# Merge and output projection for the sample's tiles first, the sample's top-k in two half lists beside the prompt's merge

## The reference, cut to what matters

```python
h  = RMSNorm(x) * (1 + scale1) + shift1
[qA|kA|vA|qB|kB|vB|gA|gB] = h @ w_in
oA = global GQA(...)  @ w_branch_a      # 8 heads of 64
oB = windowed GQA(...) @ w_branch_b
x  = x + gate1 * ((sigmoid(gA) * oA + sigmoid(gB) * oB) @ w_out)      # "merge", "output projection"
h2 = RMSNorm(x) * (1 + scale2) + shift2
# expert choice, each group routed as one set, 16 experts, cap = 2 n / 16 (32 and 128 tokens):
aff = softmax(h2 @ w_router);  g, idx = top_k(aff.T, cap)
hid = silu(h2[idx] @ w_e_gate) * (h2[idx] @ w_e_up)                  # D_FF = 2048
x  = x + gate2 * scatter_add(idx, (hid @ w_e_down) * g)
y  = RMSNorm(x)
```

## Time and profile before

| | us |
|---|---|
| Median of 3 runs (lowest, highest) | 2573.92 (2571.49, 2574.54) |
| The profiled execution | 2572.49 |
| Its span in the trace | 2570.7 |
| PE busy | 2384.8 (93%) |
| DVE busy | 1605.4 (62%) |
| ACT busy | 1162.8 (45%) |
| POOL busy | 1123.0 (44%) |
| Mean DMA rate | 199 GB/s |

### The profile page before, as it was taken

One profiled execution on the slowest core, in us unless ns is written; L12 is line 12 of the kernel. 1 busy time (PEld: TensorE's weight loads), 2 busy tenths in 40 slices (PEclk: granted clock), 3 DMA queues, 4 the chain that ended last, 5 costly groups with the idle time before them and its releaser, 6 DMA issues.

```text
span 2570.7 us, 53875 instructions
## 1 busy us (share of the span) xinstructions
PE 2384.8 (93%) x23508; PEld 1712.8 (67%) x23508; DVE 1605.4 (62%) x2014; ACT 1162.8 (45%) x1468; POOL 1123.0 (44%) x721
## 2 busy tenths in 40 slices
PE   8999899998999999934899999999999999999993
PEld 3444477655555555523788888888888888888871
DVE  1643466556111125575888878887888878887862
ACT  2111455567111112330656655665556655556552
POOL 0000111146232331042657667776677666676640
PEclk9999899999999999956999999999999999999997
DMA  8100300220221103252889998999899998999965
GB/s 315 33 17 1 115 1 1 99 99 2 82 50 50 25 34 115 99 207 76 300 317 330 324 318 321 326 336 320 312 331 318 343 315 317 331 330 326 315 234 188
DMA packets 230113, 512.23 MB, mean 199 GB/s; under 512 B 7819, under 2 KB 35580, under 8 KB 229756
## 3 DMA queue, kind: packets, MB, share of 16 engines
q1 hardware_dynamic: 219324, 477.36, 52.3%
q0 software_dynamic: 10560, 31.46, 4.4%
HBM read 480.49 MB, written 28.31 MB: 198 GB/s over the span
## 4 chain that ended last, share of the span: by engine, by line
PE 85%; DVE 6%; POOL 2%; SPq 2%; ACT 1%; DMA 1%; issue 1%; DVEq 0%; POOLq 0%; ACTq 0%
PE ps L1403 21%; PE ps L1404 20%; PE ps L1405 20%; PE ps L1472 7%; PE ps L1688 4%; PE ps L1533 3%; PE ps L1545 3%; PE ps L1514 2%; DVE arena L1054 1%; DVE ti_s L1063 1%; DVE top_s L1062 1%; DVE arena L1064 1%; POOL arena L679 1%; PE ps L1625 1%; POOL arena L676 1%
## 5 line engine op out<-in xcount | busy, mean ns | idle before, releaser
L1403 PE MATMUL ps<-arena 128*128 128x160 bf16 (+2 forms) x5344 | 1308.6, 264 | 21.8 <-DVE arena L1335 8.3
L1404 PE MATMUL ps<-arena 128*128 128x160 bf16 (+2 forms) x5344 | 1308.6, 264 | 0.0
L1405 PE MATMUL ps<-arena 128*128 128x160 bf16 (+2 forms) x5344 | 1308.4, 264 | 0.0
L1302 DVE TENSOR_TENSOR arena<-arena 128x2048 bf16<-128x2048 f32 x376 | 919.2, 2450 | 193.3 <-ACT arena L803 192.3
L803 ACT ACTIVATE arena<-arena 128x2048 bf16<-128x2048 f32 x384 | 726.7, 1904 | 239.0 <-PE ps L1405 176.9
L1403 PEld LDWEIGHTS ps<-arena 128*128 128x128 bf16 x5344 | 524.1, 98 | 154.6 <-issue 27.0
L1405 PEld LDWEIGHTS ps<-arena 128*128 128x128 bf16 x5344 | 524.3, 98 | 127.8 <-issue 1.9
L1404 PEld LDWEIGHTS ps<-arena 128*128 128x128 bf16 x5344 | 524.3, 98 | 118.9 <-issue 1.4
L727 POOL TENSOR_TENSOR arena<-arena 128x320 bf16<-128x320 f32 x128 | 283.8, 2217 | 10.0
L724 POOL TENSOR_TENSOR arena<-arena,ones 128x320 bf16<-128x320 f32 x128 | 179.4, 1401 | 179.3 <-DVE arena L1335 179.0
L991 ACT ACTIVATE arena<-ps 128x160 f32<-128x160 f32 x256 | 77.4, 303 | 351.4 <-PE ps L1405 351.4
(11 more groups left out here) (197 smaller groups left out, 2377.8 us busy)
## 6 DMA issues: line engine op xcount, KB each, us to landing
arena<-w_e_gate SPq DMA_DIRECT2D x64, 2048.0 KB, 9.1
arena<-w_e_up SPq DMA_DIRECT2D x64, 2048.0 KB, 9.5
arena<-w_e_down SPq DMA_DIRECT2D x64, 2048.0 KB, 9.2
arena<-w_ada SPq DMA_DIRECT2D x12, 2048.0 KB, 8.6
arena<-x_sample SPq DMA_DIRECT2D x16, 512.0 KB, 3.5
arena<-w_in SPq DMA_DIRECT2D x16, 512.0 KB, 5.3
arena<-w_in SPq DMA_DIRECT2D x3, 2048.0 KB, 21.0
arena<-w_out SPq DMA_DIRECT2D x2, 2048.0 KB, 8.0
```

The costliest lines, as they stand in the source:

```text
L1302: ve.tensor_tensor(lo, stage_half(kind, a), hi, ALU.subtract).then_inc(lo_done, 1)
L1403: pe.matmul(out, w_hi, x_hi, start=start, stop=False)
L1404: pe.matmul(out, w_hi, x_lo, start=False, stop=False)
L1405: return pe.matmul(out, w_lo, x_hi, start=False, stop=stop)
```

## The change

- The merge runs for the sample's tiles alone (`M, m, 0` and `M, m, 1`, 512 tokens each), then the sample's eight output projections, with all that follows each of them. Positions p = 0 to 9 stand for the tiles 2 to 9, 0, 1 (`tile_at`).
- The prompt's merge becomes steps `M2, m, b` (b = 0, 1 for the two branches) after the sample's projections, each 36 matmuls 256 wide with one sigmoid and one product. For it all eight weight tiles are loaded and split a second time (`WS, 8` to `WS, 15`): two within the sample's projections, six within the prompt's merge. Of these second splits POOL makes the low half of 2048 columns and DVE that of 1024.
- The sample's affinities lie as two lists of 512 columns, on partitions 0 to 15 and 32 to 47. The sixteen rounds (`KR`) run over 64 partitions x 512, two or three after each of the prompt's merge steps from m = 2 on. `KM` makes one list of the two sorted ones: the largest 128 are the elementwise larger of the first list and the second read backwards.
- Four `GT` steps move from the end into the prompt's merge steps m = 3 and 4.
- Two expert chunks are loaded within the prompt's merge; the first eight low halves are made by DVE, four before and four after it modulates expert 0's rows. POOL's loop for them is gone.
- The layouts of `qT`, `oT`, `hTs` and `mergedS` change so that the two groups lie apart.

The diff, cut to its core:

```diff
         s.append(("M", m, 0))
         if m + 1 < KD:
             s.append(("WS", m + 1))
-        s.append(("M", m, 1))
         if m == KD - 1:
             s += [("WO", 0), ("WO", 1)]
-        s.append(("M", m, 2))
-    for t in range(NT + 3):
-        if t < NT:
-            s.append(("O", t))
-        if t == 0:
+        s.append(("M", m, 1))
+    ns = NT - PT_TILES
+    for p in range(ns):
+        s.append(("O", p))
+        if p == 0:
             s += [("GT", n) for n in range(4)]
-        if 0 <= t - 1 < NT:
-            s.append(("X2", t - 1))
-        if 0 <= t - 2 < NT:
-            s.append(("RT", t - 2))
-        if 0 <= t - 3 < NT:
-            s.append(("AT", t - 3))
-        if t == 6:
-            s.append(("K", 0))
-        if t < NT:
-            s.append(("XO", t))
-    s += [("GT", n) for n in range(4, 8)]
-    s += [("K", 1), ("I",)]
+        if p >= 1:
+            s.append(("X2", p - 1))
+        if p >= 2:
+            s.append(("RT", p - 2))
+        if p >= 3:
+            s.append(("AT", p - 3))
+        s.append(("XO", p))
+        if p in (1, 3):
+            s.append(("WS", KD + p // 2))
+    tail = {(0, 1): [("X2", ns - 1), ("RT", ns - 2), ("AT", ns - 3)], (1, 0): [("RT", ns - 1), ("AT", ns - 2)],
+            (1, 1): [("AT", ns - 1)], (3, 0): [("GT", 4)], (3, 1): [("GT", 5)], (4, 0): [("GT", 6)], (4, 1): [("GT", 7)]}
+    r = 0
+    for m in range(KD):
+        for b in range(2):
+            s.append(("M2", m, b))
+            s += tail.get((m, b), [])
+        if m + 2 < KD:
+            s.append(("WS", KD + m + 2))
+        for _ in range((0, 0, 2, 3, 3, 3, 3, 2)[m]):
+            s.append(("KR", r))
+            r += 1
+    assert r == CAP_S // 8
+    s += [("O", ns), ("KM",), ("XO", ns), ("O", ns + 1), ("X2", ns), ("XO", ns + 1), ("RT", ns), ("AT", ns), ("X2", ns + 1),
+          ("RT", ns + 1), ("AT", ns + 1), ("K", 0), ("K", 1), ("I",)]
     return s
...
+            sp.wait_ge(mm_ready, 2 * KD)
             def load_chunk(d, c):
...
                 src = w_down[0, e].rearrange("(k p) n -> p k n", p=P)[:, 4 * DOWN[q]:4 * DOWN[q] + 4, :]
                 sp.dma_start(at(stage[kind], 4, D), src).then_inc(w_ld[kind], 16)
-            for t in range(2):
-                sp.dma_start(xo[:, t], token_rows(x_d, t)).then_inc(xo_in[t], 16)
-            for t in range(NT):
-                if t + 2 < NT:
-                    sp.wait_ge(x1_ready, t + 1)
-                    sp.dma_start(xo[:, t % 2], token_rows(x_d, t + 2)).then_inc(xo_in[t % 2], 16)
+            for p in range(2):
+                sp.dma_start(xo[:, p], token_rows(x_d, tile_at(p))).then_inc(xo_in[p], 16)
+            sp.wait_ge(wos_ready, 4)
+            mw_load(KD)
+            for p in range(NT - 2):
+                sp.wait_ge(x1_ready, p + 1)
+                sp.dma_start(xo[:, p % 2], token_rows(x_d, tile_at(p + 2))).then_inc(xo_in[p % 2], 16)
+                if p == 1:
+                    sp.wait_ge(ws_done, KD + 1)
+                    sp.wait_ge(ws_rest, 1)
+                    mw_load(KD + 1)
+            for k in range(2, KD):
+                sp.wait_ge(ws_done, KD + k)
+                sp.wait_ge(ws_rest, k)
+                mw_load(KD + k)
+                if k in (3, 4):
+                    sp.wait_ge(out_done, NT - PT_TILES)
+                    load_chunk(-1, k - 3)
             sp.wait_ge(out_done, NT)
-            load_chunk(-1, 0)
-            load_chunk(-1, 1)
             load_chunk(0, 2)
             for n, c in enumerate((3, 4, 6, 7, 9, 10)):
...
+                if k == "WS" and s[1] >= KD:
+                    m = s[1]
+                    gp.wait_ge(ws_hi, m + 1)
+                    w = half_words(mws2[m % 2], 2, MW)[:, :, 0:2 * KD * P]
+                    gp.tensor_tensor(w[:, 1], at(mw, 2 * KD * P), w[:, 0], ALU.subtract).then_inc(ws_rest, 1)
...
-            for h in range(AHEAD):
-                gp.wait_ge(hi_done, h + 1)
-                kind, slot = ring(first_half(h))
-                hi, lo = split_half(slot, h % 2)
-                gp.tensor_tensor(lo, stage_half(kind, h % 2), hi, ALU.subtract).then_inc(lo_done, 1)
             for b in range(2):
...
+                        ac.wait_ge(m_done, 2 * KD)
+                    elif m > KD:
+                        ac.wait_ge(m2_done, 2 * (m - KD) - 2)
                     ac.wait_ge(mw_in[m % 2], 96 * (m // 2 + 1))
-                    ac.activation(half_words(mws[m % 2], 2, MW)[:, 0], at(mw, MW), ACT.Copy).then_inc(ws_hi, 1)
+                    ac.activation(half_words((mws if m < KD else mws2)[m % 2], 2, MW)[:, 0], at(mw, MW), ACT.Copy)\
+                        .then_inc(ws_hi, 1)
                 if k == "WO":
                     h = s[1]
                     ac.wait_ge(wo_in[h], 16)
...
+                        ac.activation(sig[:, n % 2, b], ps[:, 4 * (n % 2) + b], ACT.Sigmoid).then_inc(sig_ready, 1)
+                if k == "M2":
+                    n, b = merge_part(s)[0], s[2]
+                    ac.wait_ge(m2_done, 2 * s[1] + b + 1)
+                    ac.wait_ge(merged_ready, n - 1)
+                    ac.activation(sig[:, n % 2, b, 0:SEQ], ps[:, 2 * (n % 2) + b, 0:SEQ], ACT.Sigmoid).then_inc(sig_ready, 1)
...
+                link(ve.max(v, a))
+                ve.max_index(ti[b][0:rows, r * 8:r * 8 + 8], v, a)
+                link(ve.match_replace(a, v, a, -1.0))
+            def merge_halves():
+                def backward(x):
...
+                first, pos = top[1][0:NE], tif[1][0:NE]
+                pick = late[0:NE, 2]
+                ve.tensor_tensor(pick, first, v, ALU.is_ge)
+                link(ve.tensor_tensor(pos, pos, f, ALU.subtract))
+                link(ve.tensor_tensor(pos, pos, pick, ALU.mult))
+                ve.tensor_tensor(first, first, v, ALU.max)
+                link(ve.tensor_tensor(pos, pos, f, ALU.add))
+            def topk_prompt():
+                for r in range(CAP_P // 8):
+                    top_round(0, r, affP[:])
+                link(ve.tensor_copy(tif[0][:], ti[0][:]))
+                ve.tensor_copy(top4, top[0][:].unsqueeze(1).to_broadcast([NE, 4, CAP_P]))
+                for g in range(4):
+                    ins = ve.tensor_scalar(tif4[:, g], tif[0][:], 4.0, float(g), ALU.mult, ALU.add)
+                link(ins)
                 ve.engine_nop().then_inc(topk_ready, 1)
             ve.memset(relb, NEG).then_inc(chain, 1)
             count[0] += 1
...
-                    w = half_words(mws[m % 2], 2, MW)
-                    ve.tensor_tensor(w[:, 1], at(mw, MW), w[:, 0], ALU.subtract).then_inc(ws_done, 1)
+                    a = 0 if m < KD else 2 * KD * P
+                    w = half_words((mws if m < KD else mws2)[m % 2], 2, MW)[:, :, a:]
+                    ve.tensor_tensor(w[:, 1], at(mw, MW)[:, a:], w[:, 0], ALU.subtract).then_inc(ws_done, 1)
                 if k == "WO":
                     h = s[1]
                     for q in range(2):
...
+                if k == "M2":
+                    n, b = merge_part(s)[0], s[2]
+                    ve.wait_ge(sig_ready, 2 * n + b + 1)
+                    x = sig[:, n % 2, b, 0:SEQ]
+                    ins = ve.tensor_tensor(x, x, ps[:, 2 * (n % 2) + b, SEQ:2 * SEQ], ALU.mult)
+                    if b:
+                        ins.then_inc(mm_ready, 1)
...
                 if k == "AT":
                     t = s[1]
                     b, free = job(s)
-                    if t < PT_TILES:
-                        dst = affP[:, t * P:(t + 1) * P]
+                    if t < NT - PT_TILES:
+                        if t == 0:
+                            link(ve.memset(affS, -1.0))
+                        dst = affS[32 * (t // 4):32 * (t // 4) + NE, t % 4 * P:(t % 4 + 1) * P]
...
-                if k == "K":
-                    topk(s[1], affP[:] if s[1] == 0 else affS)
+                if k == "KR":
+                    top_round(1, s[1], affS)
+                if k == "KM":
+                    merge_halves()
+                if k == "K" and s[1] == 0:
+                    topk_prompt()
                 if k == "I":
...
+            for h in range(4):
+                split_low(*ring(first_half(h)), h % 2, h + 1)
             for n in range(3):
                 modulate_rows(0, n, 0, first=True)
+            for h in range(4, AHEAD):
+                split_low(*ring(first_half(h)), h % 2, h + 1)
...
+                    t0 = PT_TILES + 4 * c
                     for b in range(2):
                         wb = [half_words(o + KD * P + NPAIR * P // 2 * b, NPAIR, P) for o in part]
-                        out = ps[:, 4 * (n % 2) + 2 + b, 0:w].rearrange("p (t q) -> p t q", q=P)
+                        out = ps[:, 4 * (n % 2) + 2 + b].rearrange("p (t q) -> p t q", q=P)
                         for kk in range(NPAIR):
                             ins = split_product(out, [x[:, kk, :] for x in wb],
-                                                [oT[:, NPAIR * b + kk, 4 * c:4 * c + w // P, q * P:(q + 1) * P]
```

(50 more changed lines are left out.)

145 lines of the change are left out of this document (70 added, 75 removed).

## The result

The changed kernel takes **2581.28 us** (median of 7 runs, 2580.34 to 2582.36), the kernel before 2573.92 (7 runs, 2570.56 to 2575.8): ratio 1.0032, 95% interval 1.0021 to 1.0042. It is slower, by about 7 us; forecast were 8 us less. The profiled executions lie 9.9 us apart, with spans of 2580.5 and 2570.7 us. Expert 0's first matmul stands at 1208.71 instead of 1198.96, 9.75 us later, and from there to the end both kernels need the same (1371.8 and 1371.7 us), so the whole difference lies ahead of it.

What follows compares the result with a forecast made beforehand. PE runs without a gap from expert 0's first matmul, so its start sets the end: merge start 998.8 + merge 126.5 + projections, tail, top-k 44.8 + turn 21.5 gives 1191.6, 7.4 us earlier. Forecast 2566 us, range 2552 to 2582.

Steps and rivals of the forecast that it cites:

- the turn: From the prompt's top-k end to expert 0's first matmul: 21.5 us forecast, 16.6 before, with DVE's low halves as the path.
- the prediction's signs of being wrong: Prompt's merge under 110 or over 135 us, POOL's 2048-wide subtraction over 6, turn over 28, or a longer expert 0.
- The rival that ends on the other side: At the turn to the experts, each of POOL's six row splits waits for a low half, +12.3 us: 2579, chance 0.17.
- The load turn: In the prompt's merge, one staging buffer makes load and splits run in series: 8.2 + 2.8 + 1.1 + 4.1 = 16.2 us.
- The detour: At m = 3 and 4, `GT` waits for DVE's diagonals and holds ACT's next weight copy: merge 126.5 us, 113 without cost.
- A single turn of the loop: One load, ACT high half, DVE and POOL low halves in the prompt's merge: 16.2 us, against 7.8 of PE.
- POOL's 2048-wide low half beside DVE's: In the prompt's merge, POOL's 4.06 us low half gives way to DVE's 1024 columns, so 1.1 us is added.
- that rival: Two to three rounds hold POOL's low half back at m = 4 to 7, +21 us: 2587, chance 0.05.
- The start of the merge: The prompt's merge begins at 998.8 us, after the sample's merge ends at 894.7 and its projections follow.
- Projections, tail and prompt's top-k: Between the prompt's merge and the turn: two projections 20.7 us, last tile's tail 17.9, top-k 6.2; 44.8 in all.
- The clock: PE's granted clock drops after idle stretches, adding 3.5 us to the last step of the prompt's merge.
- The rival asked for 0.50 throughout: PE's granted clock stays at 0.50 from m = 3 on and in the first projection, +5 us: 2571, chance 0.20.

## Why the prediction was wrong

**The step that failed is the turn**, in the sentence "A gather issued while DVE splits weights is a step that I price at nothing above, for it ends before DVE is through with its four low halves". The prediction took DVE's four low halves as the path and everything else as lying beside them. They took 8.9 us, as assumed, but they keep POOL from its two index copies as well as from the gathers: 5.5 us, shown by the kernel in which DVE waits. The rows then needed 7.15 us, not 3.73, since the low halves had released two 2 MB loads, one after the second and one after the fourth: shown by the kernel in which the chunks wait. No rival had this part. The last split met two low halves (4.0), not one (2.45). Forecast was 4.9 more than before; it is 12.7 by the prediction's own measure (29.3 against 16.6). Of the prediction's signs of being wrong two came: a turn over 28 us, and an expert 0 that takes longer than before (67.8 us to expert 1's first matmul against 67.0).

The rival that ends on the other side named this place and 2579, by the wrong sum: it had all six splits held and the gather at 0.5 in place of 5.5, and a chance of 0.17. The Trainium skill spoke against me here ("SBUF — State Buffer", section on SBUF's two separate sides): of a GpSimd instruction that reads SBUF and a DVE one with two SBUF inputs, the one that starts first has the shared port pair for its whole length. Trace and experiment agree, index copies of 32x1 included (2.06 us beside a low half, 0.18 without). I should have asked which instructions of POOL stand behind a low half, not only the large ones.

**The load turn was mis-sized, in three of six.** This is a term of the sum, not the mechanism. "8.2 us with the signal" was read from a load that had the queues to itself. The load of m = 2, issued beside row writes and an x load, took 13.2 us until ACT's copy; those of m = 3, 4 and 7 took 10.2, 8.4 and 10.6. With m = 3's weights ready at 44.3 us into the merge instead of 37.4, all that follows is 6 to 8 late, and the end is 6.8 late. Most of it is the load of m = 2: asked for early, it makes the merge 5.8 us shorter and the kernel 4.9 faster. Why those of m = 3 and 7 took so long stays open. In five other kernels that load m = 3, 4 and 7 in the same way they took 8.2 to 9.4 us, beside the same chunk load for m = 3; and no other load was issued beside m = 7's, in the changed kernel either.

**What held.** The detour: 13.5 forecast; taking it out shortened the merge by 14.8, 11 to 13 of them in the two turns that hold it. A single turn of the loop: 16.2 forecast, 16.3 to 17.0 measured without the detour. The round on 512 columns: 2.15 forecast, 2.16 measured; POOL's 2048-wide low half beside DVE's: 5.16 forecast, 5.10 measured, and never held by a round, so that rival falls. The start of the merge lies within its scatter. Projections, tail and prompt's top-k came within 0.8 us of the forecast. The clock: after its last idle stretch PE's granted clock was 0.50 in 1123 to 1126, 0.60 in 1126 to 1128 and 1.00 from there on, so that m = 7's 72 matmuls took 9.8 us, 2.0 more than at full clock, where 3.5 were allowed. The rival asked for 0.50 throughout and in the first projection too; the mean over the merge was 0.82, so it falls. The sign came out wrong because a gain of 7.4 us stood on 193 us of forecast path (126.5 + 44.8 + 21.5), of which two terms were read from rows that nothing disturbed.

**One part was never asked about.** The prediction compared two whole kernels. The half lists alone, at the old place, win 20 us at no other cost; the rest of the change, as it stands, spends 60 to save 33.

## What to carry to other kernels

Where work is moved beside a chain, price each link of the chain (small copies and the issue of gathers included) by a row with that neighbour, and list which loads the moved instruction releases and what else is on the queues then. In a loop of load, split and use with one staging buffer, the turn is the sum of its links, and a second delay in it hides what the removal of the first would bring: test both together before judging either. Take a change apart before pricing it as a whole: a cheap part may carry the gain and an expensive one hide it until its own waits are taken out.

## What the runs showed of the hardware

- A tiny instruction waits as long as a large one for the pair that DVE and POOL share: POOL's copy of 32x1 took 2.06 us beside a low half of DVE, 0.18 without; in the other direction DVE's copy of 16x128 took 3.97 us beside POOL's subtraction, 0.21 without. MAX8, FIND_INDEX8 and MATCH_REPLACE8 on 64x512 were never held (0.67 to 0.69 us each, beside POOL's subtractions too).
- Rows of the second gather took 3.7 to 3.85 us from its issue until they had landed with quiet queues, and 7.15 with a 2 MB load issued 3.4 us ahead of it and another 1.0 us behind.
- A round of top-k went by its columns: 3.75 us for 16x1024, 1.34 for 16x256, and 2.16 for 64x512, where a straight line between the other two gives 2.14, though it has four times the partitions.
